# Expert items of two sizes in strict alternation, a small one as the loop's body, and another slot for the first expert units

## What is computed

```
h = layer_norm(x)
for l in 0, 1:
    y = token_mixers(h, l, ...)          # diff., stick-breaking and forgetting attention, gated
    h = layer_norm(ALPHA * h + y)
    if l == 0: y = swiglu(h, w_gate, w_up, w_down)                 # dense, D_FF = 3584
    else:      y = sum over e of combine[:, e] * swiglu(h, expert e)   # top 2 of 8 experts
    h = layer_norm(ALPHA * h + y)
```

## Time and profile before

| | us |
|---|---|
| median of 3 runs | 1752.26 (1751.57 to 1752.74) |
| profiled execution, its own time | 1753.56 |
| its span, first to last instruction | 1751.8 |
| TensorE matmuls busy | 1589.9 (91%) |
| VectorE busy | 959.7 (55%) |
| ScalarE busy | 752.2 (43%) |
| DMA queue q1, share of 16 engines' span | 67.4% |
| mean granted TensorE clock | 0.945 of full |

### The profile page before, as it was taken

How to read it: one execution, slowest core, us unless ns; L and a number is a source line. 1 busy time by engine, 2 the same in 40 slices (tenths; PEclk the granted TensorE clock), 3 DMA queues, 4 the chain that set the end, 5 groups by cost and what they waited for, 6 DMA issues and landing times.

```text
span 1751.8 us, 18220 instructions
## 1 busy us (share of the span) xinstructions
PE 1589.9 (91%) x7354; PEld 1148.1 (66%) x7354; DVE 959.7 (55%) x853; ACT 752.2 (43%) x713; POOL 32.5 (2%) x30
## 2 busy tenths in 40 slices
PE   5999886899994999985599999999999999988995
PEld 4887765788883887764488635885368843325884
DVE  5547555454555536544699514983169920104986
ACT  3456543344332346652177303772057710003772
POOL 0000030000000000011000000000000000000000
PEclk9988898999996988988699999999999999999998
DMA  8442253455551353243499899999999999999970
GB/s 309 145 168 97 73 192 122 166 192 180 187 190 69 121 183 109 85 153 150 197 367 372 336 424 424 424 425 400 424 424 425 425 406 424 424 426 424 424 315 24
DMA packets 66515, 473.99 MB, mean 271 GB/s; under 512 B 7952, under 2 KB 7952, under 8 KB 9600
## 3 DMA queue, kind: packets, MB, share of 16 engines
q1 hardware_dynamic: 65488, 467.16, 67.4%
q0 software_dynamic: 944, 5.68, 0.9%
HBM read 471.76 MB, written 1.05 MB: 270 GB/s over the span
## 4 chain that ended last, share of the span: by engine, by line
PE 76%; DVE 9%; DMA 7%; ACT 4%; issue 2%; SPq 2%; ACTq 0%; DVEq 0%; POOLq 0%
PE ps L1423 20%; PE ps L1424 19%; PE ps L1425 19%; PE ps L1705 8%; DMA raw_a<-in_w_item 6%; PE ps L1739 2%; DVE lo_a L927 2%; PE ps L1679 2%; SPq L549 2%; PE ps L1668 1%; ACT w_hi L624 1%; PE ps L1712 1%; DVE h L953 1%; DVE h L954 1%; PE ps L1448 1%
## 5 line engine op out<-in xcount | busy, mean ns | idle before, releaser
L927 DVE TENSOR_TENSOR lo_a<-raw_a,w_hi 128x2048 fp32r<-128x2048 f32 (+2 forms) x117 | 252.4, 2158 | 336.7 <-ACT w_hi L624 336.2
L624 ACT ACTIVATE w_hi<-raw_a 128x2048 fp32r<-128x2048 f32 (+2 forms) x117 | 210.2, 1798 | 357.4 <-PE ps L1425 334.9
L1423 PE MATMUL ps<-w_hi,act_hi 128*128 128x512 f32 (+1 forms) x704 | 286.4, 407 | 17.1 <-DVE act_lo L965 8.5
L1424 PE MATMUL ps<-lo_a,act_hi 128*128 128x512 f32 (+1 forms) x704 | 280.2, 398 | 0.0
L1425 PE MATMUL ps<-w_hi,act_lo 128*128 128x512 f32 (+1 forms) x704 | 279.2, 397 | 0.0
L1237 DVE TENSOR_TENSOR lo_b<-raw_b,w_hi 128x2048 fp32r<-128x2048 f32 x84 | 191.9, 2290 | 25.3 <-ACT w_hi L842 24.9
L1237 DVE TENSOR_TENSOR lo_a<-raw_a,w_hi 128x2048 fp32r<-128x2048 f32 x81 | 184.4, 2289 | 29.4 <-ACT w_hi L842 28.4
L842 ACT ACTIVATE w_hi<-raw_b 128x2048 fp32r<-128x2048 f32 x84 | 161.5, 1924 | 70.5 <-PE ps L1425 70.5
L1423 PE MATMUL ps<-w_hi,x_hi 128*128 128x512 f32 x448 | 179.4, 400 | 10.0 <-DVE lo_a L1237 5.2
L842 ACT ACTIVATE w_hi<-raw_a 128x2048 fp32r<-128x2048 f32 x81 | 155.4, 1918 | 67.3 <-PE ps L1425 63.1
L1425 PE MATMUL ps<-w_hi,x_lo 128*128 128x512 f32 x448 | 177.2, 396 | 0.0
(11 more groups left out here) (253 smaller groups left out, 1901.8 us busy)
## 6 DMA issues: line engine op xcount, KB each, us to landing
raw_a<-in_w_item SPq DMA_DIRECT2D x210, 1024.0 KB, 14.2
raw_b<-in_w_item SPq DMA_DIRECT2D x168, 1024.0 KB, 18.7
raw_a<-in_w_mix SPq DMA_DIRECT2D x60, 1024.0 KB, 4.9
raw_a<-in_w_mix SPq DMA_DIRECT2D x8, 512.0 KB, 3.6
ln_gb<-in_ln_mix POOLq DMA_DIRECT2D x2, 1024.0 KB, 4.8
cst<-in_consts SPq DMA_DIRECT2D x1, 1494.0 KB, 10.5
h<-in_x SPq DMA_DIRECT2D x1, 1024.0 KB, 5.0
ln_gb<-in_ln_in POOLq DMA_DIRECT2D x1, 1024.0 KB, 10.7
```

The source lines that it names most:

```text
L624: nc.scalar.activation(w_hi[:, q % HRING, 0:n], raw(slot)[:, 0:n], ACT.Copy).then_inc(s_hi, 1)
L927: nc.vector.tensor_tensor(w_lo(slot)[:, 0:n], raw(slot)[:, 0:n], w_hi[:, q % HRING, 0:n].bitcast(F32), ALU.subtract).then_inc(s_lo, 1)
L1423: nc.tensor.matmul(dst, xh, wh, start=start, stop=False)
L1424: nc.tensor.matmul(dst, xh, wl, start=False, stop=False)
```

## The change

1. `KIND` becomes B S B S B S B S, with `POS_RANK` so that big positions still have the ranks 0 to 3 and small ones the ranks 4 to 7. The seventh written-out item is big; the loop's item is small.
2. Overflow items are small as well (64 tokens), so an expert can overflow twice: a second capacity row `cap2` (capacity plus 64) is added, and the overflow part of the table is computed over 16 candidates (`TWICE`) instead of 8.
3. `slot_of` maps the first expert units to the `raw_a` slots in the order in which mixer 1 leaves them: expert unit k < 7 of every fourteen goes to slot (114 + k) mod 7.
4. `ring_b_at` is rounded down to a multiple of 64 instead of 32: 171968. `small` shrinks from 2000 to 1792 words, `rt` grows from 632 to 824.

```
-KIND = "BSBSBSSB"
-POS_RANK = [0, 7, 1, 6, 2, 5, 4, 3]
+KIND = "BSBSBSBS"
+POS_RANK = [0, 7, 1, 6, 2, 5, 3, 4]
-OVER = 4
+OVER, TWICE = 4, 2 * N_EXP
+    put("cap2", np.array([CAP[k] + CAP["S"] for k in KIND])[None, :])

 def slot_of(g):
-    return g % SLOTS_A if g < MOE_BASE else (g - MOE_BASE) % SLOTS
+    if g < MOE_BASE:
+        return g % SLOTS_A
+    k = (g - MOE_BASE) % SLOTS
+    return (MOE_BASE + k) % SLOTS_A if k < SLOTS_A else k

-        ring_b_at = (top - (SLOTS - SLOTS_A) * 8192) // 32 * 32
+        ring_b_at = (top - (SLOTS - SLOTS_A) * 8192) // 64 * 64
-        small = place("small", [P, 2000])
+        small = place("small", [P, 1792])
-        rt = place("rt", [P, 632])
+        rt = place("rt", [P, RT])
...
         class Item:
-                self.bigs = bigs_before(i) if turn is None else turn + bigs_before(i)
-                self.smalls = i - bigs_before(i)
+                self.bigs = bigs_before(i)
+                self.smalls = i - self.bigs if turn is None else turn + (i - self.bigs)
...
             def x_big(self):
-                return True if self.turn is not None else BIG[self.n + 1]
+                return self.turn is None and BIG[self.n + 1]
...
             pick(ov, cnt)
-            link(nc.vector.tensor_tensor(ov, ov, c("cap"), ALU.is_gt))
-            link(nc.vector.tensor_tensor_scan(inc, ov, ov, 0.0, ALU.add, ALU.max))
-            link(nc.vector.tensor_tensor(exc, inc, ov, ALU.subtract))
-            o48 = [P, OVER, N_EXP]
...
-            link(nc.vector.scalar_tensor_tensor(rkc, item_rk[:, :, 0:N_EXP], 1.0, cols("cap"), ALU.add, ALU.subtract))
+            nc.vector.tensor_tensor(ov2[:, 0:N_EXP], ov, c("cap"), ALU.is_gt)
+            nc.vector.tensor_tensor(ov2[:, N_EXP:TWICE], ov, c("cap2"), ALU.is_gt)
+            for i, name in enumerate(("cap", "cap2")):
+                o = N_EXP * i
+                nc.vector.scalar_tensor_tensor(rkc[:, :, o:o + N_EXP], item_rk[:, :, 0:N_EXP], 1.0, cols(name), ALU.add, ALU.subtract)
+                nc.vector.tensor_copy(cwc[:, :, o:o + N_EXP], item_cw[:, :, 0:N_EXP])
+                ins = nc.vector.tensor_copy(fic[:, o:o + N_EXP], ftab[:, 0:N_EXP])
+            link(ins)
+            link(nc.vector.tensor_tensor_scan(inc, ov2, ov2, 0.0, ALU.add, ALU.max))
+            link(nc.vector.tensor_tensor(exc, inc, ov2, ALU.subtract))
+            o4 = [P, OVER, TWICE]
...
```

More of the change, by code:

```diff
@@ L63, in group_width @@
     return 1024 if g < 3 else 512
+RT = 824
 GROUPS = [("diff", 1), ("sb", 1), ("fox", 1), ("diff", 0), ("sb", 0), ("fox", 0)]
@@ L83 @@
 for _name, _n in (("ident", P), ("tri", TILES * SEQ), ("iota", P), ("iota64", P), ("iota8", N_EXP),
-                  ("first", N_EXP), ("tie", N_EXP), ("posrank", N_EXP), ("cap", N_EXP), ("overj", OVER),
+                  ("first", N_EXP), ("tie", N_EXP), ("posrank", N_EXP), ("cap", N_EXP), ("cap2", N_EXP), ("overj", OVER),
                   ("mfox1", 256), ("mfox0", 128),
@@ L328, in build @@
         lg_row = scratch(SEQ)
-        assert used[0] <= 2000
+        assert used[0] <= 1792, used[0]
         rused = [0]
@@ L361, in build @@
         ov = route(N_EXP)
[L362 to L366, removed]
+        inc = route(TWICE)
+        exc = route(TWICE)
+        ov2 = route(TWICE)
+        rkc = by_tile(TWICE)
+        cwc = by_tile(TWICE)
+        fic = route(TWICE)
+        osel = route(OVER * TWICE).rearrange("p (a b) -> p a b", a=OVER)
+        oprod = route(OVER * TWICE).rearrange("p (a b) -> p a b", a=OVER)
         item_rk = by_tile(POSITIONS + 1)
@@ L369, in build @@
         ftab = route(POSITIONS + 1)
-        assert rused[0] <= 632, rused[0]
+        assert rused[0] <= RT, rused[0]
         itab = ctx.enter_context(nc.sbuf_tensor("itab", [P, 16], I32))
@@ L489, in split @@
             def split(self, k):
-                q = SPLIT_INDEX[self.at + k]
-                return q if self.turn is None else self.turn * ITEM_UNITS + q
+                return SPLIT_INDEX[self.at + k]
             def loads(self, k):
@@ L500, in hi_free @@
             def hi_free(self, k):
-                if self.turn is None:
-                    return SPLIT_UNITS[SPLIT_INDEX[self.at + k] - HRING] + 1
-                return self.unit(k - HRING + 1)
+                return SPLIT_UNITS[SPLIT_INDEX[self.at + k] - HRING] + 1
             def x_big(self):
-                return True if self.turn is not None else BIG[self.n + 1]
+                return self.turn is None and BIG[self.n + 1]
         def groups_of(kind, t):
@@ L1379, in _ @@
             pick(ov, cnt)
[L1380 to L1387 removed]
+            nc.vector.tensor_tensor(ov2[:, 0:N_EXP], ov, c("cap"), ALU.is_gt)
[9 more added lines that the diff above has]
+            o4 = [P, OVER, TWICE]
+            link(nc.vector.tensor_tensor(osel, exc.unsqueeze(1).to_broadcast(o4), c("overj").unsqueeze(2).to_broadcast(o4), ALU.is_equal))
+            link(nc.vector.tensor_tensor(osel, osel, ov2.unsqueeze(1).to_broadcast(o4), ALU.mult))
             def pick_over(dst, values):
[L1390 removed]
+                link(nc.vector.tensor_tensor(oprod, osel, values.unsqueeze(1).to_broadcast(o4), ALU.mult))
                 link(nc.vector.tensor_reduce(dst, oprod, AX, ALU.add))
@@ L1394, in _ @@
                 pick_over(item_rk[:, t, N_EXP:POSITIONS], rkc[:, t, :])
-                pick_over(item_cw[:, t, N_EXP:POSITIONS], item_cw[:, t, 0:N_EXP])
-            pick_over(ftab[:, N_EXP:POSITIONS], ftab[:, 0:N_EXP])
+                pick_over(item_cw[:, t, N_EXP:POSITIONS], cwc[:, t, :])
+            pick_over(ftab[:, N_EXP:POSITIONS], fic)
             link(nc.vector.tensor_scalar(item_rk[:, :, N_EXP:POSITIONS], item_rk[:, :, N_EXP:POSITIONS], -1.0, None, ALU.add))
-            link(nc.vector.tensor_scalar(ftab[:, 0:1], inc[:, N_EXP - 1:N_EXP], 1.0, None, ALU.add))
+            link(nc.vector.tensor_scalar(ftab[:, 0:1], inc[:, TWICE - 1:TWICE], 1.0, None, ALU.add))
             nc.vector.tensor_copy(itab[:, 0:POSITIONS + 1], ftab).then_inc(s_tab, 1)
```

## The result

| | before | after |
|---|---|---|
| median | 1752.5 (1751.57 to 1757.35, 4 runs) | 1722.07 (1720.93 to 1726.95, 4 runs) |
| profiled execution; its span | 1753.56; 1751.8 | 1722.11; 1720.3 |
| mean granted TensorE clock | 0.945 | 0.949 |

The kernel takes 0.9826 of the time before, 95% interval 0.98 to 0.9852: a gain of 1.7%, clear of zero and under 2%. Run again later beside three experiments, the same kernel gave 0.9834 (0.9821 to 0.9848). Every ratio in this document is to executions of the kernel before that were taken beside it, not to the 1752.5 of the table. Predicted were 1719.5 us and a gain of 32.75; the profiled spans differ by 31.45.

The account below looks back on a forecast made before the run. Transfers and TensorE were both taken as near their limit, with idle time at the front and end. −10.2 + 0.75 − 23.0 + 0.5 − 0.8 = −32.75 took the profiled 1753.56 to 1720.8, median 1719.5 us; range 1714 to 1726.

Parts of the forecast that it names:

- Front: End of mixer 1: first expert units in slots already free, so ScalarE's split stops waiting for a landing; −10.2 us.
- Table: Routing before item 0: wider and additional table instructions on VectorE lie on the path; +0.75 us, bounds 0.3 and 1.7.
- End: Last two items: big then small, at gather intervals 125.57 and 84.61, with a shorter tail; −23.0 us together.
- Loop entry: Loop around the last, small item: entry costs between 0 and 2.3 us, taken as +0.5; per-unit register cost nil.
- Ring: Loads into `raw_b`, start moved 32 bytes to a multiple of 64: shorter TensorE waits at small-to-big turns; −0.8 us.
- 1: Ring limits earlier, at the end: the final small item meets late weights; 1726 to 1732 us, chance 0.07.
- 2: Front gain swallowed: item 0 waits for something else, such as VectorE's table; 1729.7 us, chance 0.04.
- 3: Ring's boundary worth more: turns lose their 1.50 us each, sparing TensorE 1.2 GHz; 1711 to 1714 us, chance 0.08.
- 4: Slower: the loop runs twice, for an added small overflow item priced at 84.6 us; 1804 us, chance 0.01.
- 5: Loop's small items paced by register waits on each landing, 0.2 us a unit and more; 1728 and up, chance 0.03.
- what would show it: Expected signs in the new profile, among them addition near 816.3, item 0 near 858.5, gathers 125.6 and 84.6 apart.
- bounds of the terms: Spread of the sum: routing +1, entry +1.8, boundary −1.3 or +0.8, front ±1, given as 1715.5 to 1723.5 us.

Follow-up runs that it names:

- e2: The kernel before with the new `slot_of` only; measured 1742.58 us, ratio 0.9929 to the kernel before.
- e6: The kernel before with `small` 8 words shorter, moving what lies behind it by 32 bytes; 1757.69 us, ratio 1.0019 to the kernel before.
- a0: The changed kernel once more, unaltered, as partner for later runs; 1723.36 us, ratio 0.9834 to the kernel before.
- e4: The changed kernel with `ring_b` on a multiple of 256 bytes (171776) and `RT` 648; 1717.73 to 1725.93 us in five of six executions, ratio 0.9822.
- e5: The changed kernel with both paddings to 256 bytes, shared area of mixer and items and `ring_b`; 1714.29 us, ratio 0.9794 to the kernel before.
- e8: The changed kernel with the loop's count raised by one, a second pass over an empty item; 1828.49 us, ratio 1.0419 to the kernel before.

## Why the prediction was right, point by point

- **Front, −10.2.** Measured −9.95 by itself (`e2`). Layer 0 was the right model of layer 1 without the wait, to 0.3 us. From the same split the addition L1148 comes 817.53 − 801.30 = 16.23 us later, against 15.92 in layer 0 and 26.10 in layer 1 before; it stands at 817.53 instead of the expected 816.3 by that 0.3 and because the split itself is 0.89 later (801.30 against 800.41). Item 0 started at 859.74, expected near 858.5, for the same reason.
- **Table, +0.75.** Measured 0.77. The unlinked pitch, guessed at 0.07, is 0.08.
- **End, −23.0.** The gathers came 125.48 and 84.50 us apart instead of 125.57 and 84.61; items 6 and 7 take 23.24 less. Right in mechanism and size.
- **Loop entry, +0.5.** Nothing: the first unit of the looped small item takes 1.88 us, that of a static one 1.88. It is the lower end of the bounds. A small item needs no `lo_a`, so nothing is waited for there.
- **Ring, −0.8.** Wrong in its mechanism, shorter waits. The prediction set a 64-byte boundary against a coarser one and took a value between. Measured are 2.483 us a unit instead of 2.492, and waits at the turns of 1.33, 1.99 and 1.78 us in place of 1.43, 1.50 and 2.30: nothing that could be told from zero. `raw_b` was to run at 428 GB/s if 64 bytes decide, and ran at 424. The prediction read the Trainium skill's rule as no gain; by the beats counted above it is one of 263, 0.01 us a unit (an estimate), and 0.009 was measured. The start on 256 bytes, which the change doesn't have, shortens the waits. What the 32 bytes of `ring_b` did bring is elsewhere: the products of `lo_b`, 694 ns a triple before and 687 after, 336 times, 2.3 us.
- **Not in the sum: the addresses.** The prediction looked at the 32 bytes of `ring_b`, which the diff names, and not at `small` and `cst`, which move everything behind them. That costs 3.3 us (`e6`, where such a shift stands alone), of which `lo_b`'s 2.3 are to be taken off. This is the step that failed, by omission.
- **Not in the sum: a turn with the clock down.** At 1278.24 TensorE had waited 1.99 us, and 1.2 us later its products slow from 0.39 to 0.63 us for some 3 us, at a granted clock of 0.50 (1280 to 1282.7), which is 1.2 GHz. It cost 1.6 us in this run; in `a0` no turn had it, in the kernel before the last one. Timeline of the kernel after:
```profile
1279.46 0.52 PE L1440 MATMUL ps<-w_hi,x_lo 128*128 128x512 f32 x1
1279.78 0.63 PE L1438 MATMUL ps<-w_hi,x_hi 128*128 128x512 f32 x1
...
1283.33 0.39 PE L1438 MATMUL ps<-w_hi,x_hi 128*128 128x512 f32 x1
```
- **The rivals.** 1 fell: the small item at the end meets its weights in time, no wait for a DMA is left. 2 fell with `e2`. 3 didn't occur: the change hasn't the boundary that counts. Its mechanism holds where the ring has it: in `e4` and `e5` the turns are shorter and the clock fell at none. But they lose 0.1 to 1.0 us of their wait against the kernel before, and not all 1.50; that `e5` measured 1714.29, near the 1711 to 1714 named there, is for the larger part the pace of the products. 4 didn't occur, and its price is 103 us and not 84.6, as `e8` shows: the prediction priced a second small item without its wait for the loads, which it had read as 103.10 in the kernel before. 5 fell: 84.50 us in the loop.

- **Signs and bounds.** One sign of "what would show it" failed: no stretch without transfers was to be longer than 10 us before the last gather, and from 841.1 to 853.4 us there is none, 12.3 us (0 GB/s in 842 to 853). It was at odds with the prediction's own front, where the ring is full by about 840 and item 0 starts near 858.5, and it costs nothing. And the bounds of the terms as given add up to 1716.2 to 1724.1, not 1715.5 to 1723.5.

The sum was right by 1.3 us in the span: 2.4 omitted, less the 1.1 by which the stretch of front, table and item 0 did better in this run. In `a0` that stretch took 167.92 instead of 165.26 us. The difference is the clock in routing and at item 0's start, as windows of the kernel after and then of `a0` show:
```profile
837.00:843.00 6.00, 5.26 (x36) 3.53 (x33) 0.98 (x5) 0.37 (x1) 0.00 (x0) 0.81 0.56 232
...
861.00:867.00 6.00, 6.00 (x23) 4.80 (x23) 0.63 (x1) 1.92 (x1) 0.00 (x0) 0.82 0.23 71
```
```profile
837.00:843.00 6.00, 6.00 (x31) 3.69 (x30) 0.95 (x4) 0.00 (x0) 0.00 (x0) 0.52 0.59 244
...
861.00:867.00 6.00, 5.04 (x13) 4.00 (x14) 0.85 (x2) 0.00 (x0) 0.00 (x0) 0.53 0.01 3
```
So the nearness is partly luck; each large term is confirmed by a run of its own.

## What to carry to other kernels

Where two kinds of work share a prefetch ring, one faster than its loads and one slower, alternate them and end with the kind whose tail is the shorter; two fast ones in a row run at the loads' pace. A slot's number is free to choose: give the first loads of a new phase the slots that are freed first. And when a change resizes any buffer, look at where everything behind it now starts: keep the targets of large transfers and the operands of matmuls on multiples of 256 bytes, the one start of those measured here that cost nothing.

## What the runs showed of the hardware that I had not expected

- **A matmul's pace depends on where its operand starts.** fp32r products of 512 columns start 227 ns apart when the operands start on a multiple of 256 bytes, so three take 681. With the loaded operand (`mrg`, `dhid`) 224 past such a multiple, three take 700 (`after`, `e6`). With the streamed one (`lo_b`) there, in one of the three products, they take 694 (`before`); 192 past, 687 (`after`); on 256, 681 (`e4`, `e5`). Other starts weren't measured. The busy time in the rows (0.39 or 0.40) hardly shows it; the starts do. The plain fp32 products of the small items show none of it: such an item takes 82.6 us in the kernel before, in the one after and in `e5`, with `raw_b` 224, 192 and 0 past.
- **A load's pace depends on where it writes in SBUF:** 2.44 us a megabyte aligned to 256 bytes, 2.48 and 2.49 when 192 and 224 past.
- **Short waits differ in their price.** Each of the twelve profiled kernels has three turns. At the 21 where TensorE waited 1.78 us or less the clock stayed up. Of the 15 with 1.93 us or more, nine were followed by products at 0.63 us, and the item's first unit took 6.3 to 6.9 us; at the other six it took 5.1 to 5.3, and 4.3 behind a wait of 1.32. So cutting a wait from 2.3 to 1.3 us is worth 1 us or 2.6. What makes the nine differ from the six can't be read from these runs.
